# First convolution taps on ScalarE, and keys and up products on tiles without the norm's root, in a two-model kernel of exact fp32 products

## The chip, the cores and the metric

The kernel runs on one core of a Trainium2 chip. The metric is the device time in microseconds of one execution; a profiled execution also gives the span from the first to the last instruction. TensorE (PE) multiplies, VectorE (DVE), ScalarE (ACT) and GpSimd (POOL) do the rest, and SyncE (SP) issues the weights' transfers.

## The reference, cut to what matters

Two models are computed one behind the other on 256 tokens of width 1024. The first has two layers, each with a mixer (multi-head latent attention, then a short convolution) and a mixture of 32 experts, of which every token takes two:

```python
def expert_block(args):
    xb, e = args
    return (jax.nn.silu(xb @ w_gate[e]) * (xb @ w_up[e])) @ w_down[e]
```

The second has a state-space mixer and a dilated attention, each followed by an FFN with a causal depthwise convolution of width 3 over the tokens. The attention's keys and values come from a norm of their own:

```python
def _rms_norm(x, w, eps=RMS_EPS):
    xf = x.astype(jnp.float32)
    y = xf * lax.rsqrt(jnp.mean(xf * xf, axis=-1, keepdims=True) + eps)
    return (y * w.astype(jnp.float32)).astype(x.dtype)

def _conv_ffn(h, w_up, conv_w, w_down):
    u = _causal_depthwise_conv(h @ w_up.astype(h.dtype), conv_w)
    gate, val = u[..., :FFN_DIM], u[..., FFN_DIM:]
    return (jax.nn.silu(gate) * val) @ w_down.astype(h.dtype)

...
k_sh, v_sh = _shared_kv(x, kv_norm, w_kv, positions)
x = x + _dilated_mixer(_rms_norm(x, b_norm[j]), k_sh, v_sh, att_w_q[j], att_w_o[j], positions)
x = x + _conv_ffn(_rms_norm(x, ffn_norm[layer]), ffn_w_up[layer], ffn_conv_w[layer], ffn_w_down[layer])
```

## The kernel before

The program is a chain of stages, each a class with one method per engine: `Start`, `Mla`, `Moe` 0, `Conv`, `Moe` 1, `Ssm`, `Ffn` 0, `Dilated`, `Ffn` 1, `Finish`. Each engine runs its methods in the order in which the code is written; semaphores order the engines among each other. There is no scheduler.

The activations lie transposed in SBUF: `X` is 8 tiles of 128 features by the 256 tokens. Where fp32 must be exact, a value is split into a high part, rounded to the PE's fast format, and a low part, the rest; a product is then three fast products (high by high, low by high, high by low; `product3`, L584; `first_linear3_tensor`, L618 to L624). ACT rounds (`round_scalar`, L297) and DVE makes the rest (`rest_vector`, L303), for weights as for values. A weight chunk is 128 partitions by 4096 elements, and goes through a ring of six slots that SP fills in order; a slot is free when the products that read it are done.

A norm at a seam goes: DVE adds the stage's output to `X`, ACT squares (L432, L479), POOL adds squares up (L487), PE sums over partitions with ones (L495, L497), ACT takes the root (L652), DVE its reciprocal `rstd` (L657), then values times gain times `rstd` (L661), rounded by ACT (L680), lows by DVE (L668). Only then does the next stage's first product start.

`Moe`: after the routing's ranks (L1393) PE opens four accumulator banks with products of zeros (`open_tensor`, L1344), gathers the tokens of expert team 0 (L1307; its operands are the rounded turned x and its lows, L1578), and then takes the 32 experts in turn (gate and up L1328 and L1337, result L1352, into the accumulators). At the end comes a branch for experts with more tokens than fit, after which `more_begin` and so on would run.

`Ffn`: 11 up chunks, each two tiles m of 128 gate and 128 value columns. For each tile ACT evicts the products from PSUM (L2744 for the first two tiles, L2749 for the others) into `PB`, DVE does the convolution: first tap (L2783), two further taps (L2786), for both halves; ACT does the silu (L2726), POOL the product with the value half (L2808), ACT rounds it (L2728), POOL makes its low part (L2810). In `scalar` the steps stand in this order:

```python
for m in range(KFF):
    if m % 2 == 0:
        (self.w_up + self.w_down)[m // 2 + 1].round_scalar(e, w)
    if m >= 2:
        make_h(m - 2)
...
    if m >= 4:
        w.wait_ge(*dve.at(key, "taps", m - 4))
```

`make_h` is the silu, the wait for POOL's product and its rounding; the eviction of tile m comes behind it.

`Dilated`: keys of three pairs of heads (`keys`, from chunks `w_kv[0]`, `w_kv[1]`), values (`tokens`), rotary position turns (a PE product, L2894, then three DVE operations, L3130 to L3133), then the heads' queries, scores and outputs.

Of the kernel before, what the change touches and what calls it, by code (L numbers as in the profile page):

```python
# [16 lines left out]
P = 128  # L17
# [3 lines left out]
HALF = SLOT // 2  # L21

# [479 lines left out]
class Kernel:  # L502
# [102 lines left out]
    def first_linear3_tensor(self, e, w, chunk, outs, weights, values, n_k, tiles, pieces=False):  # L605
# [6 lines left out]
        for i in range(n_k):  # L612
# [4 lines left out]
            for out, name, cols in outs:  # L617
                e.matmul(out, high(i, cols).bitcast(F32R), values[0](i).bitcast(F32R), start=i == 0, stop=False)  # L618
                end = e.matmul(out, low(i, cols).bitcast(F32R), values[0](i).bitcast(F32R), start=False, stop=False)  # L619
        end.then_inc(*pe.up("free", chunk.number))  # L620
# [43 lines left out]
    def norm_parts_vector(self, e, w, tag, value, gain, high, low, chunk=None):  # L664
# [5 lines left out]
        for k in range(KD):  # L670
            self.norm_value_vector(e, w, tag, k, value, gain)
            if chunk and k % 2 and k > 1:
                chunk.rest_piece_vector(e, w, k // 2)
# [13 lines left out]
    def modulated_parts_vector(self, e, w, tag, layer, T, high, low, chunk=None):  # L687
# [9 lines left out]
        for k in range(KD):  # L697
# [3 lines left out]
            if chunk and k % 2 and k > 1:  # L701
                chunk.rest_piece_vector(e, w, k // 2)
# [514 lines left out]
class Moe:  # L1217
    def __init__(self, k, layer, T, cap, before):
# [12 lines left out]
        self.slots, self.zero = ar.take(P), ar.take(P)  # L1231
        self.zeros_by = k.mats[:, 0:4, :].rearrange("p m n -> p (m n)")
# [31 lines left out]
    def sync(self, e, w):  # L1264
# [8 lines left out]
        self.k.ring.close_halves()  # L1273
        self.more_sync(e, w)
# [81 lines left out]
    def tensor(self, e, w):  # L1356
# [38 lines left out]
        w.wait_ge(*pool.at(key, "zero"))  # L1395
        for b in range(KD // 2):
            _, emptied = banks.next(dve, key, "acc", b)
            banks.hold(key, "acc", b)
            w.wait_ge(*emptied)
        self.open_tensor(e)  # L1400
# [50 lines left out]
        for part in range(KD // 2):  # L1451
            gather(0, part)
        for x in range(EXPERTS):
# [21 lines left out]
    def scalar(self, e, w):  # L1475
# [52 lines left out]
        self.then.first_chunk().round_piece_scalar(e, w, 0)  # L1528
        k.root_scalar(e, w, ("moe", layer), SEQ, eps=NORM_EPS * NORM_EPS if layer else NORM_EPS)
        self.then.first_chunk().round_piece_scalar(e, w, 1)  # L1530
        act.mark("end", key)

    def vector(self, e, w):
# [144 lines left out]
        for part, between in enumerate((weights, shared, tables, lambda: self.last_steps.close_vector(e, w))):  # L1678
            turned_x(0, part)
            between()  # L1680
# [10 lines left out]
        for x in range(EXPERTS):  # L1691
# [7 lines left out]
            if x % TEAM == TEAM - 1 and x // TEAM + 2 < EXPERTS // TEAM:  # L1699
                places_of(x // TEAM + 2)  # L1700
        w.wait_ge(*pe.at(key, "sum", EXPERTS - 1))
# [5 lines left out]
        self.then.first_chunk().rest_piece_vector(e, w, 0)  # L1707
# [1671 lines left out]
```

## Time and profile before

| what | value |
| --- | --- |
| median of 3 runs | 2243.75 us (2243.53 to 2244.0) |
| profiled execution, its own time | 2242.49 us |
| its span | 2240.7 us, mean granted TensorE clock 0.975 |
| PE busy | 2109.5 us (94%) |
| DVE busy | 1003.7 us (45%) |
| ACT busy | 718.4 us (32%) |
| POOL busy | 244.7 us (11%) |

The shares are averages over the whole program. The stages differ: the expert stages move weights nearly all the time, the FFNs keep DVE as busy as PE. The expert stages end at about 742 and 1348 us, the first FFN's up chunks run from 1644 to 1773, the attention from 1844 to 2031, and the second FFN's up chunks to 2166.

### The profile page before, as it was taken

The numbers are of one execution on the slowest core, as the hardware profiler recorded it, in microseconds if no ns is written. First come the engines' busy times: TensorE is split into PE (matmuls) and PEld (weight loads), VectorE is DVE, ScalarE is ACT, GpSimd is POOL, SyncE is SP. The second block draws the span as 40 slices with busy tenths as digits, with TensorE's granted clock in tenths as the row PEclk, the third lists the DMA queues.
The fourth block names the chain that finished last, engine by engine and source line by source line (L and its number), as shares of the span: only waits on it lengthen the run. The fifth ranks groups of instructions, "written<-read, shape, count | busy, mean of one in ns | idle before, by whom it ended". The sixth has DMA issues, their size and how long they took to land. (4 is left out here: it accounts for less than half of the span.)

```text
span 2240.7 us, 31183 instructions
## 1 busy us (share of the span) xinstructions
PE 2109.5 (94%) x13462; PEld 1481.8 (66%) x13462; DVE 1003.7 (45%) x1653; ACT 718.4 (32%) x1079; POOL 244.7 (11%) x220
## 2 busy tenths in 40 slices
PE   5999999999999898999999988997899989998998
PEld 3845744444443696444444437975899989998997
DVE  3434411111111564111111107865479846777983
ACT  3234211111111442111111118855545534444552
POOL 0000000000000000000000000046125400002540
PEclk9999899999999999999999999999999999999999
DMA  9777599999999557999999985432345454434542
GB/s 326 252 273 275 227 410 421 421 421 421 421 421 421 192 204 304 417 421 421 422 420 421 421 352 191 151 113 76 113 151 189 174 196 122 113 113 151 188 171 94
DMA packets 216208, 616.86 MB, mean 275 GB/s; under 512 B 20224, under 2 KB 107392, under 8 KB 166656
## 3 DMA queue, kind: packets, MB, share of 16 engines
q1 hardware_dynamic: 208960, 612.01, 71.0%
q10 hardware_dynamic: 7104, 2.76, 0.5%
q8 instruction: 110, 1.80, 0.3%
q14 instruction: 34, 0.28, 0.0%
HBM read 613.69 MB, written 1.05 MB: 274 GB/s over the span
## 5 line engine op out<-in xcount | busy, mean ns | idle before, releaser
L1328 PE MATMUL bank<-ring,arena 128*64 128x512 f32 x2048 | 454.4, 593 | 12.4 <-DMA ring<-in_moe_w_up 12.3
L584 PE MATMUL bank<-normed_rounded,ring_rounded 128*128 128x256 f32 x3424 | 415.5, 283 | 5.0 <-ACT normed_rounded L680 3.4
L584 PEld LDWEIGHTS bank<-normed_rounded,ring_rounded 128*128 128x128 f32 x3424 | 411.2, 189 | 6.9 <-issue 4.3
L1328 PEld LDWEIGHTS bank<-ring,arena 128*64 128x64 f32 x2048 | 149.4, 137 | 305.8 <-issue 304.9
L1674 DVE TENSOR_TENSOR arena<-arena,bank 64x512 f32<-64x512 f32 x64 | 43.6, 681 | 659.3 <-ACT arena L1498 659.3
L303 DVE TENSOR_TENSOR ring_rounded<-ring,ring_rounded 128x4096 fp32r<-128x4096 f32 (+2 forms) x66 | 286.6, 4345 | 115.2 <-ACT ring_rounded L297 115.0
L584 PE MATMUL bank<-arena_rounded,ring_rounded 128*128 128x256 f32 x2336 | 290.9, 284 | 6.8 <-ACT arena_rounded L1927 2.6
L584 PEld LDWEIGHTS bank<-arena_rounded,ring_rounded 128*128 128x128 f32 x2336 | 283.3, 190 | 9.2 <-ACT arena_rounded L1927 3.4
L297 ACT ACTIVATE ring_rounded<-ring 128x4096 fp32r<-128x4096 f32 (+2 forms) x66 | 227.7, 3450 | 39.4 <-DMA ring<-in_ffn_w_down 32.8
L1337 PE MATMUL bank<-ring,arena 128*64 128x512 f32 x1024 | 233.8, 598 | 3.8 <-ACT arena L1505 3.8
L1498 ACT ACTIVATE arena<-bank 64x512 f32<-64x512 f32 x64 | 38.1, 596 | 451.0 <-PE bank L1328 451.0
L1337 PEld LDWEIGHTS bank<-ring,arena 128*64 128x64 f32 x1024 | 67.8, 136 | 122.4 <-issue 109.6
L572 PEld LDWEIGHTS bank<-mats,arena 128*128 128x128 f32 (+2 forms) x662 | 85.0, 167 | 78.8 <-issue 66.5
L1352 PE MATMUL bank<-arena 64*128 64x256 f32 x1024 | 127.8, 388 | 1.4 <-ACT arena L1512 1.4
L1512 ACT ACTIVATE arena<-bank 128x512 f32<-128x512 f32 x64 | 38.3, 599 | 275.2 <-PE bank L1337 275.2
L572 PE MATMUL bank<-mats,arena 128*128 128x128 f32 (+2 forms) x662 | 102.9, 278 | 8.5 <-POOL arena L2414 5.4
L1352 PEld LDWEIGHTS bank<-arena 64*128 64x128 f32 x1024 | 93.2, 186 | 23.7 <-issue 11.6
L2786 DVE SCALAR_TENSOR_TENSOR arena<-arena,cols 128x256 f32<-128x256 f32 x176 | 94.4, 537 | 6.3
L2810 POOL TENSOR_TENSOR arena_rounded<-arena,arena_rounded 128x256 fp32r<-128x256 f32 x44 | 93.5, 2125 | 23.3 <-ACT arena_rounded L2728 23.3
L1307 PE MATMUL bank<-arena_rounded 128*128 128x256 f32 x512 | 78.4, 298 | 0.0
L1307 PEld LDWEIGHTS bank<-arena_rounded 128*128 128x128 f32 x512 | 65.7, 190 | 5.0 <-issue 1.2
L1505 ACT ACTIVATE arena<-bank 128x256 f32<-128x256 f32 x64 | 24.7, 386 | 132.5 <-PE bank L572 132.5
(274 smaller groups left out, 2101.4 us busy)
## 6 DMA issues: line engine op xcount, KB each, us to landing
ring<-in_moe_w_gate SPq DMA_DIRECT2D x128, 1024.0 KB, 16.6
ring<-in_moe_w_up SPq DMA_DIRECT2D x128, 1024.0 KB, 18.7
ring<-in_moe_w_down SPq DMA_DIRECT2D x128, 1024.0 KB, 18.4
ring<-in_w_mod SPq DMA_DIRECT2D x24, 2048.0 KB, 11.8
ring<-in_ffn_w_up SPq DMA_DIRECT2D x44, 1024.0 KB, 6.9
ring<-in_ssm_w_in SPq DMA_DIRECT2D x12, 2048.0 KB, 8.3
ring<-in_ffn_w_down SPq DMA_DIRECT2D x10, 2048.0 KB, 8.0
ring<-in_conv_w_in SPq DMA_DIRECT2D x6, 2048.0 KB, 9.1
```

The costliest lines, as they stand in the source:

```text
L297: e.activation(ring.rounded[(self.number + 1) % RING][:, 0:n].bitcast(F32R), ring.slots[self.number % RING][:, 0:n], ACT.Copy).then_inc(*s ...
L303: e.tensor_tensor(ring.rounded[slot][:, 0:n].bitcast(F32R), ring.slots[slot][:, 0:n], ring.rounded[(self.number + 1) % RING][:, 0:n], ALU. ...
L572: return e.transpose(out, in_, self.mats[0:rows, 0, 0:rows])
L584: end = e.matmul(out, lhs.bitcast(F32R), rhs.bitcast(F32R), start=start and n == 0 and k == 0, stop=stop and n == 2 and k == n_k - 1)
L1307: end = e.matmul(out, f[:, t, feats].bitcast(F32R), mine[:, t, hot].bitcast(F32R), start=t == 0 and f is self.f_high, stop=t == self.NT - ...
L1328: ends[i] = e.matmul(bank[rows, :], xt[:, n * KD // 2 + j, :], weights[:, j, :], start=n == 0 and j == 0, stop=n == 1 and j == KD // 2 - 1)
L1337: end = e.matmul(bank[n * cap:(n + 1) * cap, :], self.ht[x][:, k, :], weights[:, i, n * 512:(n + 1) * 512], start=k == 0, stop=k == KF - 1)
L1352: end = e.matmul(self.acc(kk), self.y[x][rows, i * P:(i + 1) * P], self.back[x][rows, :], start=False, stop=last and kk % 2 == 1)
L1512: e.activation(self.y[x % 2], banks.of(key, "y", x)[:, :], ACT.Copy).then_inc(*act.up(key, "y", x))
L1674: e.tensor_tensor(h, h, banks.of(key, "h", x)[0:cap, :], ALU.mult).then_inc(*dve.up(key, "h", x))
L2786: e.scalar_tensor_tensor(buf, self.PB[:, s, j, q:q + T], w3[:, q:q + 1], buf, ALU.mult, ALU.add).then_inc(*dve.up())
L2810: e.tensor_tensor(self.H_low[:, m, :].bitcast(F32R), self.H[:, m, :], self.H_high[:, m, :], ALU.subtract).then_inc(*pool.up(key, "h low", m))
```

## The change

Five edits.

1. **Opening of the experts.** The zero products use a rounded zero (one fast pass each instead of several) and stand behind the gathers; DVE makes all turned tiles of team 0 before the routing weights.
2. **End of the experts.** The next stage's first chunk is fetched before the branch, ACT rounds its pieces 0 and 1 before the squares, DVE makes their rests around them. The loop for overfull experts is one loop instead of three.
3. **Seams into both FFNs.** The first two up chunks multiply `raw` = X times gain, without the root. Their rows take `rstd` at the eviction, which DVE does (`normed`). The sum of squares is closed inside the first product.
4. **First tap of the convolution** by ACT, after the eviction, as a copy with a scale per partition.
5. **Dilated attention.** The keys and values multiply raw tiles as well; keys take `rstd` at their eviction (`normed(n)`), values a scale by token (`by_token`), which PE turns from `rstd` (`roots`).

```diff
@@ Moe.tensor @@
-        w.wait_ge(*pool.at(key, "zero"))
...
-        self.open_tensor(e)
...
         for part in range(KD // 2):
             gather(0, part)
+        w.wait_ge(*pool.at(key, "zero"))
...
+        self.open_tensor(e)
@@ Moe.open_tensor @@
+        zero = self.zero_rounded.bitcast(F32R)
         for b in range(KD // 2):
-            e.matmul(self.k.banks.of(self.key, "acc", b)[:, :], self.zero, self.zeros_by, start=True, stop=False)
+            e.matmul(self.k.banks.of(self.key, "acc", b)[:, :], zero, across(zero, BANK // P), start=True, stop=False)
@@ Moe.scalar @@
+        for q in (0, 1):
+            self.then.first_chunk().round_piece_scalar(e, w, q)
...
         self.more_scalar(e)
-        self.then.first_chunk().round_piece_scalar(e, w, 0)
         k.root_scalar(e, w, ("moe", layer), SEQ, eps=NORM_EPS * NORM_EPS if layer else NORM_EPS)
-        self.then.first_chunk().round_piece_scalar(e, w, 1)
@@ Ffn.raw_vector @@
+    def raw_vector(self, e, w, m):
+        e.tensor_scalar(self.raw[:, m, :], k.X[:, m, 0:SEQ], k.col("ffn_norm")[:, self.layer, m:m + 1], None, ALU.mult
+                        ).then_inc(*k.dve.up(self.key, "raw value", m))
...
@@ Ffn.tensor @@
-        k.first_linear3_tensor(e, w, first, outs, (high, low), self.x_parts, KD, k.norm_tiles(key))
+        k.first_linear3_tensor(e, w, first, outs, (high, low), self.raw_parts, KD, self.raw_ready,
+                               between=lambda i: self.prior.close_tensor(e, w) if i == 1 else None)
@@ Ffn.scalar @@
-            if m % 2 == 0:
+            if m == 0:
+                self.w_up[2].round_scalar(e, w)
+            elif m % 2 == 0 and m > 2:
                 (self.w_up + self.w_down)[m // 2 + 1].round_scalar(e, w)
             if m >= 2:
                 make_h(m - 2)
...
+            w.wait_ge(*(act if m >= 4 else dve).at(key, "up", m))
+            for j in range(2):
+                e.activation(self.acc[:, s, j, :], self.PB[:, s, j, 0:T], ACT.Copy,
+                             scale=taps[:, self.layer, j * KFF + m, 0:1]).then_inc(*act.up(key, "tap", m, j))
@@ Ffn.vector @@
+            w.wait_ge(*act.at(key, "tap", m))
             for j in range(2):
                 buf, w3 = self.acc[:, s, j, :], taps[:, self.layer, j * KFF + m, :]
-                e.tensor_scalar(buf, self.PB[:, s, j, 0:T], w3[:, 0:1], None, ALU.mult).then_inc(*dve.up())
@@ Dilated.tensor @@
-        keys(0, False)
-        keys(1, True)
+        first_keys()
+        roots()
+        last_keys()
         rotary(("k", 0))
-        keys(2, False)
         rotary(("k", 1))
         tokens(self.w_kv[1], slice(256, 512), 0)
         rotary(("k", 2))
@@ Dilated.vector @@
-        self.w_kv[1].rest_vector(e, w)
         rotary(("k", 0))
+        rotary(("k", 1))
         self.w_kv[2].rest_vector(e, w)
-        rotary(("k", 1))
+        normed(2)
         rotary(("k", 2))
```

On ACT, in the FFN's loop (one weight chunk's rounding at L297, then two tiles), the rows before are:

```order
L297 ACTIVATE ring_rounded<-ring 128x4096
L2726 ACTIVATE arena<-arena 128x256
L2728 ACTIVATE arena_rounded<-arena 128x256
L2749 ACTIVATE arena<-bank 128x2x256
L2726 ACTIVATE arena<-arena 128x256
L2728 ACTIVATE arena_rounded<-arena 128x256
L2749 ACTIVATE arena<-bank 128x2x256
```

and after, where the rounding has line 298, silu 2783, rounding of the product 2785 and the eviction 2802:

```order
L298 ACTIVATE ring_rounded<-ring 128x4096
L2783 ACTIVATE arena<-arena 128x256
L2785 ACTIVATE arena_rounded<-arena 128x256
L2802 ACTIVATE arena<-bank 128x2x256
L2806 ACTIVATE arena<-arena,cols 128x256 x2
L2783 ACTIVATE arena<-arena 128x256
L2785 ACTIVATE arena_rounded<-arena 128x256
L2802 ACTIVATE arena<-bank 128x2x256
L2806 ACTIVATE arena<-arena,cols 128x256 x2
```

Behind every eviction stand two copies with a column as scale, ahead of the next silu; nothing else in the loop has moved.

On PE, at the opening of an expert stage, behind the ranks, before and after (L1344 and L1350 are the zero products, L1307 and L1312 the gather, L1328 and L1333 the first expert's gate and up):

```order
L1390 MATMUL bank<-arena,mats 128x32
L1393 MATMUL bank<-arena,mats 128x32 x2
L1344 MATMUL bank<-mats,arena 128x512 x4
L1307 MATMUL bank<-arena_rounded 128x256 x32
L1328 MATMUL bank<-ring,arena 64x512 x16
```

```order
L1396 MATMUL bank<-arena,mats 128x32
L1399 MATMUL bank<-arena,mats 128x32 x2
L1312 MATMUL bank<-arena_rounded 128x256 x32
L1350 MATMUL bank<-arena_rounded 128x512 x4
L1333 MATMUL bank<-ring,arena 64x512 x16
```

The gather has changed places with the zero products.

On DVE, at the entry of the dilated attention (L3130 to L3133 before and L3278 to L3281 after are a rotary, L303 and L304 the rest of a weight chunk, L3257 and L3262 after are `normed`), before and after:

```order
L668 TENSOR_TENSOR normed_rounded<-normed,normed_rounded 128x256 x8
L661 SCALAR_TENSOR_TENSOR arena<-residual,cols,rstd 128x256 x8
L668 TENSOR_TENSOR arena_rounded<-arena,arena_rounded 128x256 x8
L303 TENSOR_TENSOR ring_rounded<-ring,ring_rounded 128x4096
L3130 TENSOR_TENSOR residual<-bank,residual 32x2x256
L3131 TENSOR_TENSOR arena<-arena,residual 32x512
L3133 TENSOR_TENSOR arena<-arena,residual 32x512
L303 TENSOR_TENSOR ring_rounded<-ring,ring_rounded 128x4096
L3130 TENSOR_TENSOR residual<-bank,residual 32x2x256
L3131 TENSOR_TENSOR arena<-arena,residual 32x512
L3133 TENSOR_TENSOR arena<-arena,residual 32x512
L3130 TENSOR_TENSOR residual<-bank,residual 32x2x256
```

```order
L304 TENSOR_TENSOR ring_rounded<-ring,ring_rounded 128x4096
L3257 TENSOR_TENSOR arena<-bank,rstd 128x256 x4
L3268 COPY arena<-bank 128x2
L3278 TENSOR_TENSOR residual<-bank,residual 32x2x256
L3279 TENSOR_TENSOR arena<-arena,residual 32x512
L3281 TENSOR_TENSOR arena<-arena,residual 32x512
L3278 TENSOR_TENSOR residual<-bank,residual 32x2x256
L3279 TENSOR_TENSOR arena<-arena,residual 32x512
L3281 TENSOR_TENSOR arena<-arena,residual 32x512
L304 TENSOR_TENSOR ring_rounded<-ring,ring_rounded 128x4096
L3262 TENSOR_TENSOR arena<-bank,rstd 128x512
L3278 TENSOR_TENSOR residual<-bank,residual 32x2x256
```

The lows of the queries (L668 before, L3318 after) stand behind the rotaries now, and `normed(2)`, L3262, stands between the third chunk's rest and the third rotary.

## Rows read from the trace of the kernel before

**Rows 1.** The page's costliest groups (busy us, mean ns, idle before, releaser).
```profile
L1328 PE MATMUL bank<-ring,arena 128*64 128x512 f32 x2048 | 454.4, 593 | 12.4 <-DMA ring<-in_moe_w_up 12.3
...
L2786 DVE SCALAR_TENSOR_TENSOR arena<-arena,cols 128x256 f32<-128x256 f32 x176 | 94.4, 537 | 6.3
```

**Rows 2.** Timeline (start, duration, engine line op), PE, two openings of the experts.
```profile
264.79 6.65 PE L1344 MATMUL bank<-mats,arena 128*128 128x512 f32 x8 [1.90 <-DVE arena_rounded L1578]
270.87 4.47 PE L1307 MATMUL bank<-arena_rounded 128*128 128x256 f32 x32
...
870.33 5.96 PE L1344 MATMUL bank<-mats,arena 128*128 128x512 f32 x8 [1.90 <-DVE arena_rounded L1578]
```

**Rows 3.** Windows (PE, PEld, DVE, ACT, POOL busy, PE clock, DMA share, GB/s), first opening.
```profile
265.00:270.00 5.00, 5.00 (x6) 1.94 (x7) 0.44 (x3) 0.00 (x0) 0.00 (x0) 0.50 1.01 423
270.00:275.00 5.00, 5.00 (x34) 4.25 (x33) 2.40 (x7) 0.00 (x0) 0.00 (x0) 0.92 0.13 54
```

**Rows 4.** Timeline, ACT, the ends of the first and second expert stage.
```profile
746.37 1.28 ACT L312 ACT_TABLE_LOAD   x1 [0.79 <-issue]
...
1354.22 1.06 ACT L312 ACTIVATE ring_rounded<-ring 128x1024 fp32r<-128x1024 f32 x1 [1.38 <-DMA ring<-in_ssm_w_in]
```

**Rows 5.** Timeline, PE, from the state-space stage into the first FFN.
```profile
1639.99 0.70 PE L497 MATMUL bank<-rstd,mats 128*128 128x256 f32 x2 [0.53 <-ACT rstd L479]
...
1658.08 2.18 PE L584 MATMUL bank<-normed_rounded,ring_rounded 128*128 128x256 f32 x17
```

**Rows 6.** Timeline, ACT, DVE, POOL, the FFN loop's first cycle.
```profile
1658.56 3.62 ACT L297 ACTIVATE ring_rounded<-ring 128x4096 fp32r<-128x4096 f32 x1
1667.28 0.42 ACT L2728 ACTIVATE arena_rounded<-arena 128x256 fp32r<-128x256 f32 x1 [3.36 <-POOL arena L2808]
1670.17 3.63 ACT L297 ACTIVATE ring_rounded<-ring 128x4096 fp32r<-128x4096 f32 x1
...
1662.21 4.42 DVE L303 TENSOR_TENSOR ring_rounded<-ring,ring_rounded 128x4096 fp32r<-128x4096 f32 x1
...
1663.99 3.25 POOL L2808 TENSOR_TENSOR arena<-arena 128x256 f32<-128x256 f32 x1 [19.07 <-ACT arena L2726]
1668.56 0.74 POOL L2808 TENSOR_TENSOR arena<-arena 128x256 f32<-128x256 f32 x1
```

**Rows 7.** Windows, the first FFN's up chunks; timeline, DVE and POOL, a later cycle.
```profile
1658.00:1772.00 114.00, 114.00 (x963) 113.96 (x961) 109.44 (x133) 60.00 (x72) 65.74 (x40) 1.00 0.52 170
...
1731.64 4.97 DVE L303 TENSOR_TENSOR ring_rounded<-ring,ring_rounded 128x4096 fp32r<-128x4096 f32 x1
1743.09 4.97 DVE L303 TENSOR_TENSOR ring_rounded<-ring,ring_rounded 128x4096 fp32r<-128x4096 f32 x1
...
1732.86 4.35 POOL L2810 TENSOR_TENSOR arena_rounded<-arena,arena_rounded 128x256 fp32r<-128x256 f32 x1 [0.53 <-ACT arena_rounded L2728]
```

**Rows 8.** Timeline, PE, the first FFN's down products begin; ACT, a scaled copy.
```profile
1772.94 3.31 PE L584 MATMUL bank<-arena_rounded,ring_rounded 128*128 128x256 f32 x26 [0.78 <-ACT arena L2749]
...
1372.37 0.51 ACT L2324 ACTIVATE arena<-arena,cols 128x256 f32<-128x256 f32 x1
```

**Rows 9.** Timeline, PE and DVE, from the first FFN into the dilated attention.
```profile
1829.28 10.30 PE L584 MATMUL bank<-arena_rounded,ring_rounded 128*128 128x256 f32 x72 [2.11 <-DVE residual L2795]
1844.65 15.55 PE L584 MATMUL bank<-normed_rounded,ring_rounded 128*128 128x256 f32 x96 [3.40 <-ACT normed_rounded L680]
1873.14 1.02 PE L2894 MATMUL bank<-arena 128*128 128x512 f32 x2
...
1874.20 0.68 DVE L3130 TENSOR_TENSOR residual<-bank,residual 32x512 f32<-32x512 f32 x1 [3.30 <-PE bank L2894]
```

**Rows 10.** Timeline, PE, the entry of the second FFN and its down products.
```profile
2019.41 11.55 PE L584 MATMUL bank<-normed_rounded,ring_rounded 128*128 128x256 f32 x96
2051.05 2.18 PE L584 MATMUL bank<-normed_rounded,ring_rounded 128*128 128x256 f32 x17
...
2165.90 2.37 PE L584 MATMUL bank<-arena_rounded,ring_rounded 128*128 128x256 f32 x18 [0.78 <-ACT arena L2749]
```

More of the change, by code:

```diff
@@ L1677, in vector @@
             self.last_steps.step_vector(e, w, at)
-        for part, between in enumerate((weights, shared, tables, lambda: self.last_steps.close_vector(e, w))):
+        for part in range(KD // 2):
             turned_x(0, part)
-            between()
+        weights()
+        shared()
+        tables()
+        self.last_steps.close_vector(e, w)
         w.wait_ge(*dve.now())
@@ new lines, in more_tensor @@
+            with e.Fori(0, (self.n_blocks - 1) * EXPERTS, 1) as it:
+                e.wait_ge(*self.more_count("vector", it, 2))
+                awake()
+                for tile in range(KD):
+                    self.gather_tensor(e, x_turned[:, tile * self.cap:(tile + 1) * self.cap], tile, slice(0, self.cap),
+                                       self.mine[0])
+                self.back_tensor(e, turned, 0).then_inc(matmul, 1)
+                e.wait_ge(*self.more_count("vector", it, 4))
+                awake()
+                e.wait_ge(*self.more_count("landed", it, 48))
+                awake()
+                for half in range(2):
+                    tiles = slice(half * KD // 2, (half + 1) * KD // 2)
+                    end = self.gate_up_tensor(e, rows, self.rows_of(0), half, gate[:, tiles, :], up[:, tiles, :])[1]
+                end.then_inc(matmul, 1)
+                e.wait_ge(*self.more_count("vector", it, 5))
+                awake()
+                self.turn_h_tensor(e, turned, 0).then_inc(matmul, 1)
+                e.wait_ge(*self.more_count("scalar", it, 2))
+                awake()
+                self.down_tensor(e, x_turned, 0, range(KF), down).then_inc(matmul, 1)
+                e.wait_ge(*self.more_count("scalar", it, 3))
+                awake()
+                self.open_tensor(e)
+                self.sum_tensor(e, 0, True).then_inc(matmul, 1)
+                e.wait_ge(*self.more_count("vector", it, 6))
+                awake()
@@ new lines, in roots, with last_keys @@
+        def roots():
+            bank, emptied = banks.next(dve, "att root")
+            w.wait_ge(*emptied)
+            w.wait_ge(*dve.at("root", ("ffn out", 0)))
+            for c in range(2):
+                end = k.turn(e, bank[:, c * P:(c + 1) * P], k.rstd[:, c * P:(c + 1) * P])
+            end.then_inc(*pe.up("att root"))
+        def last_keys():
+            chunk = self.w_kv[1]
+            (high,), (low,) = chunk.high(), chunk.low()
+            bank, emptied = banks.next(dve, "pair", ("k", 2))
@@ L2909, in keys @@
-            if last:
-                pe.mark("free", chunk.number)
+                                  self.k_parts, KD, chunk.ready())
+            ends[2].then_inc(*pe.up("pair", ("k", 2)))
         def query(h, g):
@@ L3193, in vector @@
             k.plain_vector(e, w, "att y", m)
+            self.then.raw_vector(e, w, m)
+        for m in range(4):
+            self.then.raw_low_vector(e, w, m)
         self.then.prepare_vector(e, w)
@@ L3196, in vector @@
             k.plain_vector(e, w, "att y", m)
-        k.root_vector(e, w, "dilated out", T)
+            self.then.raw_vector(e, w, m)
+        for m in range(4, KD):
+            self.then.raw_low_vector(e, w, m)
+        for q in range(4):
+            if q == 2:
+                k.root_vector(e, w, "dilated out", T)
+            self.then.w_up[1].rest_piece_vector(e, w, q)
         dve.mark("end", "dilated")
```

256 lines of the change are left out of this document (167 added, 89 removed).

## The prediction

> **What bounds the kernel now.** I read the page's totals first, then the timelines around each place that the diff touches, then the windows of the FFN. TensorE is busy for 94% of the span (the table above), and its costliest group, the experts' gate products, idles 12.4 us, nearly all for a transfer [rows 1]: the expert stages run at the pace of the DMA late and of TensorE early, and everything else is a TensorE stage with short waits at its seams. So only two things can move the time: the seams (norms, openings), and whatever could take the FFN's up chunks away from TensorE.
>
> The FFN is the place to look at closely. Over its 114 us of up chunks PE is busy 114.00 and DVE 109.44, while ACT has 60.00 and POOL 65.74 [rows 7]. Two engines run level: one cycle (one weight chunk, two tiles) takes DVE 1743.09 - 1731.64 = 11.45 us, and PE 96 products at 11.55/96 = 0.12 us [rows 10], 11.4 to 11.5. That ACT is half idle does not mean that it has room. Its program order per tile is silu, wait for POOL's product, round the product, evict the next tile, and once a cycle a weight chunk's rounding. In the first cycle of the loop (starts 1658.56 and 1670.17) this serial chain alone takes 11.61 us [rows 6]. The reader is to see why: ACT's rounding ends, DVE starts the chunk's rest at 1662.21 for 4.42, and POOL's product, issued at 1663.99, ends only at 1667.24, 0.61 behind the rest. Unhindered the same product takes 0.74. So ACT waits 3.36 us behind a DVE operation that it has itself released [rows 6]. Later in the loop DVE is late by its own load, and the operation caught under the rest is POOL's next one, 4.35 us [rows 7].
>
> The Trainium skill says this too (SBUF — State Buffer, "Who interferes with whom"): a DVE instruction with two SBUF inputs and a GpSimd instruction that reads SBUF exclude each other for a whole instruction, and issue order decides who waits. The 4.42-us rest and the 3.25-us product agree with it.
>
> **The change, part by part.**
>
> Opening of the experts, twice. Before, PE waits 1.90 for the shared lows, does eight records of plain fp32 zeros for 6.65 us at half the clock (0.50), and only then the gather, 4.47 [rows 2, 3]. After, the gather starts as soon as its operands are there (265.3, the same release plus the copies) and runs 4.47 at full, up to 8.9 at half clock; I take a start at half clock and 6.4. Then four rounded zero products of 512 columns, twice a 256-column one: 4 x 0.24 = 0.95. That ends at 272.65, against 270.87 + 4.47 = 275.3 [rows 2]: -2.6. The second opening, 5.96 of zeros, by the same steps: -2.3. Bounds of each: 0 (the expert stream is the transfers' from there on) and -4.6 (full clock). The DMA share falls to 0.13 in the window behind the opening [rows 3], so the transfers have been waiting for slots which the products free, and move along with them; hence not 0.
>
> End of the experts, twice. A table load of 1.28 and a rounded piece of 1.06 leave the chain between squares and root [rows 4]; in their place two pieces precede the squares, which then start about 0.95 later: -1.4. At the second stage the piece also waited 1.38 for its transfer [rows 4], which now starts earlier: -2.8. Bounds: -3.7 and +1.
>
> Entries of the two FFNs. Today the root must be complete before the first product, and the first chunk ends at 1658.08 [rows 5] and 2051.05 [rows 10]. After, the products follow the out products at once. Into the first FFN: start 1639.95, 96 products 11.45, and between them the closing squares, which today end at 1639.99 + 0.70 [rows 5] and take 1.9 with their waits: 1653.3, -4.8. Into the second: out products end at 2030.96 [rows 10], + 11.55 + 1.5: 2044.05, -7.0. The 16 added raw operations per seam lie on DVE and ACT under the out products; they delay the first chunk's rest by up to 3.4 us, which the start above includes. If they cost more, the gain falls one for one.
>
> Entry of the dilated attention. The 3.40 wait and the slow products behind it (15.55 for 96, where 11.55 is the full-clock time) [rows 9, 10] go: the first keys end at 1851.7 instead of 1860.04. Then comes a new wait. DVE's order is now rotary 0, rotary 1, the rest of the third chunk, `normed(2)`, and TensorE's third rotary needs that last one. From PE's first rotary at 1857.8 (the first keys' 1851.7, the root's transposes 0.3, 48 products 5.8): two rotaries of three operations of 0.68 each (4.1; the first of today's third one stands in [rows 9]), a rest of 4.42 as in [rows 6], 0.7: 1867.9 against 1873.14 [rows 9], with TensorE idle for about 2.8. Net -5.5, between -8.3 (no wait) and -4. The tokens queued behind this rotary on PE move with it.
>
> First taps of the FFN, 44 each, from DVE to ACT. DVE loses four `TENSOR_SCALAR` a cycle. On ACT a copy with a scale column on such a tile takes 0.51 [rows 8], 0.48 of it beyond the overlap of neighbours: four a cycle are 1.92, and all of them stand in the serial chain, behind the eviction and ahead of the next silu. And relieving DVE does not take the POOL wait away, it fixes it: DVE's cycle work falls to 4.42 + 8 x 0.54 = 8.7 us [rows 1, 6], so DVE is always idle when ACT's rounding ends, its rest starts 0.03 later, and ACT's silu needs 0.4 before POOL may even start. So every cycle is as the first one of today, 11.61, plus 1.92: **13.53 us** against 11.4 of PE. TensorE, which had nothing to wait for, waits 2.1 us per chunk.
>
> For the first FFN: the rounding of the fourth up chunk ends at 1672.9 (today 1670.17 + 3.63 = 1673.8 [rows 6]). Seven cycles later, 1767.6, the last up chunk is rounded; from there to the eviction that releases the down products are one more cycle and 6.1 us, so they start at 1787.3, against 1772.94 [rows 8]: +14.35, the better entry included. The second FFN by the same steps: 2064.1 + 94.7 + 19.7 = 2178.5 against 2165.90 [rows 10]: +12.6. Behind that point nothing on the path changes.
>
> **The sum.** Openings -4.9, ends -4.2, first FFN +14.35, attention -5.5, second FFN +12.6: +12.35. The profiled execution took 2242.49, so 2254.8; the median of the runs lies 1.26 higher, so about **2256 us**. A measurement of this kernel tells about 0.2%, 4.5 us.
>
> **Rivals.**
> 1. *TensorE stays the bound in the FFNs (faster).* DVE is at 109 of 114 us and ACT at 60 [rows 7]; if only load counted, moving work from the one to the other would be free. It needs POOL's product to get in ahead of the rest. Then the chain loses about 3.4 a cycle, is 10.1, and PE sets 11.4. The time would be -9.1 - 4.8 - 5.5 - 7.0 = -26.4: 2217. Against it: the order rest, then product, is seen in [rows 6] exactly where DVE was idle. The Trainium skill speaks for this rival in words (Perfetto Trace Analysis, "Optimizing Scalar/DVE Operations": where DVE is saturated, some work may go to Scalar). By that sentence the sum would be 2217 as well; by the rows it is 2256.
> 2. *A cycle in between (no change).* Fourteen cycles count, so each 0.1 us of cycle is 1.4 us, and the sum is zero at 13.53 - 12.35/14 = 12.65 us. Taps that overlap the evictions, or some cycles of each kind, would do it: 2239 to 2248.
> 3. *TensorE loses its clock too (slower still).* Waits of 2 to 3 us have cost it: after one of 3.40 the 96 products took 4.0 more than at full clock [rows 9, 10]. With every chunk at 14.5 the sum is +12.35 + 14 x 1.0 = +26: 2270. Up to 2.1 us of it are free, since PE would only fill its own wait.
> 4. *The seams don't give what I count (slower).* If the raw operations make the out products' evictions late, -4.8 and -7.0 are lost: the FFN cycles are untouched by that only if the fourth rounding is late as well, which adds up to 10 us: 2266.
>
> **How the numbers follow.** The forecast's own case (cycle 13.1 to 14.0, seams as counted) 0.55, giving 2248 to 2264; rival 3 0.10; rival 4 0.07; rival 2 0.10; rival 1 0.18. Slower by over 0.2% is 0.55 + 0.10 + 0.07, within 0.2% 0.10, faster 0.18. The range leaves out rival 1's lower part and the end of rival 3: 2230 to 2268.
>
> **What would show it.** In the FFN of the changed kernel: DVE's 4.42-us rests 13.5 us apart with idle time before each, ended by ACT's rounding; POOL's `TENSOR_TENSOR` beside each of them at about 4.7 instead of 0.8; ACT waiting on POOL 4.7 once a cycle; PE with a wait of about 2 us per chunk; the first down product near 1778 in the new trace's time (9.1 earlier seams taken off 1787). Rests 11.4 apart with PE busy throughout would make the forecast wrong, and so would a POOL product of 0.8 that ends before the rest starts. At the attention's third rotary PE should idle nearly 3 us for DVE; at both openings the gather should start within 0.5 us of the shared lows, and the zeros take about 1 us.

## The result, and the profile after

| | before | after |
| --- | --- | --- |
| median | 2243.64 us (4 runs) | 2261.69 us (4 runs, 2258.08 to 2262.1) |
| ratio, 95% interval | | 1.008 (1.0062 to 1.0097) |
| profiled execution's span | 2240.7 us | 2259.9 us |

The changed kernel is 18 us slower, 0.8%. The forecast was 2256 in a range to 2268, slower. The page of the changed kernel, two of the costliest groups (busy us, mean ns, idle before, releaser):

```profile
L585 PE MATMUL bank<-normed_rounded,ring_rounded 128*128 128x256 f32 x3136 | 384.7, 284 | 23.9 <-DVE ring_rounded L304 22.4
...
L2896 POOL TENSOR_TENSOR arena<-arena 128x256 f32<-128x256 f32 x44 | 99.4, 2259 | 133.8 <-ACT arena L2783 133.8
```

TensorE's products on normed values now idle 22.4 us for DVE's rests; before, the same group idled 5.0, 3.4 of it for ACT:

```profile
L584 PE MATMUL bank<-normed_rounded,ring_rounded 128*128 128x256 f32 x3424 | 415.5, 283 | 5.0 <-ACT normed_rounded L680 3.4
```

POOL's product with the value half averages 2.26 us, three times its free 0.74 [rows 6].

In the changed kernel the rest of a weight chunk is L304, POOL's product L2896, its low part L2898, and the matrix products are L585. The experiments' kernels have their own numbers, some lines on from the kernel that each starts from; there DVE's rest in pieces is L312 or L313.

The FFN's cycle, timeline of ACT, DVE, POOL and PE in the changed kernel, and the start of the down products:

```profile
1675.18 3.61 ACT L298 ACTIVATE ring_rounded<-ring 128x4096 fp32r<-128x4096 f32 x1
1683.88 0.42 ACT L2785 ACTIVATE arena_rounded<-arena 128x256 fp32r<-128x256 f32 x1 [4.79 <-POOL arena L2896]
1688.64 3.61 ACT L298 ACTIVATE ring_rounded<-ring 128x4096 fp32r<-128x4096 f32 x1
...
1678.82 4.43 DVE L304 TENSOR_TENSOR ring_rounded<-ring,ring_rounded 128x4096 fp32r<-128x4096 f32 x1 [1.47 <-ACT ring_rounded L298]
1692.28 4.42 DVE L304 TENSOR_TENSOR ring_rounded<-ring,ring_rounded 128x4096 fp32r<-128x4096 f32 x1 [1.47 <-ACT ring_rounded L298]
...
1679.17 4.68 POOL L2896 TENSOR_TENSOR arena<-arena 128x256 f32<-128x256 f32 x1 [4.38 <-ACT arena L2783]
1686.11 0.75 POOL L2896 TENSOR_TENSOR arena<-arena 128x256 f32<-128x256 f32 x1 [1.00 <-ACT arena L2783]
...
1683.30 11.65 PE L585 MATMUL bank<-normed_rounded,ring_rounded 128*128 128x256 f32 x96 [1.79 <-DVE ring_rounded L304]
...
1779.33 20.90 PE L585 MATMUL bank<-arena_rounded,ring_rounded 128*128 128x256 f32 x155 [5.54 <-ACT arena L2802]
```

This is the picture which the forecast asked for. ACT rounds at 1675.18 and 1688.64: 13.46 us a cycle. Its rounding ends at 1678.79, DVE starts the rest 0.03 later, POOL's product starts at 1679.17 and takes 4.68, ending 0.60 behind the rest; ACT stands for 4.79 us. The second product of the cycle, beside no rest, takes 0.75. PE waits 1.79 for the next chunk, and 5.54 ahead of the down products (0.78 before [rows 8]).

The early seams, timeline of PE: the first opening, the first product of the convolution, and a late stretch of that stage:

```profile
263.85 6.38 PE L1312 MATMUL bank<-arena_rounded 128*128 128x256 f32 x32 [2.41 <-DVE arena_rounded L1584]
270.06 1.09 PE L1350 MATMUL bank<-arena_rounded 128*128 128x512 f32 x4
271.08 7.09 PE L1333 MATMUL bank<-ring,arena 128*64 128x512 f32 x32
...
747.07 0.55 PE L619 MATMUL bank<-normed_rounded,ring_rounded 128*128 128x256 f32 x1 [4.24 <-ACT normed_rounded L714]
...
821.25 23.49 PE L585 MATMUL bank<-arena_rounded,ring_rounded 128*128 128x256 f32 x185 [0.28 <-ACT arena_rounded L1937]
```

The gather has its 6.4 us, the zeros 1.09, as costed. From the ranks' products to the first expert it is 271.08 - 260.83 = 10.25 us against 275.27 - 261.85 = 13.42: -3.2. The other opening gives -1.5, the two ends -2.35 and -1.65 by the same reading. The last row is one that gave some back: these 185 products took 21.94 us before, now 23.49. The granted clock from 820 to 830 us is 0.83 now; before, every window over the same products shows 1.00.

From the state-space stage into the first FFN, timeline of PE and ACT:

```profile
1600.18 30.56 PE L585 MATMUL bank<-arena_rounded,ring_rounded 128*128 128x256 f32 x256 [0.41 <-DVE ring_rounded L304]
1641.09 3.95 PE L627 MATMUL bank<-arena_rounded,ring_rounded 128*128 128x256 f32 x32
...
1661.73 3.61 ACT L298 ACTIVATE ring_rounded<-ring 128x4096 fp32r<-128x4096 f32 x1
```

The out products end at 1630.74 (1639.02 before), the first up chunk at 1645.04 (1658.25 before; the row behind it in [rows 5] starts 0.17 before that end): 13.2 us ahead, of which 8.3 were there at the out products and 4.9 are the seam's. The fourth chunk's rounding ends at 1665.34 (1673.80 by [rows 6]).

Into and through the dilated attention's entry, timeline of PE and DVE:

```profile
1838.04 10.30 PE L585 MATMUL bank<-arena_rounded,ring_rounded 128*128 128x256 f32 x72 [2.19 <-DVE residual L2877]
1856.64 3.96 PE L627 MATMUL bank<-normed_rounded,ring_rounded 128*128 128x256 f32 x32
1876.98 2.08 PE L3000 MATMUL bank<-arena 128*128 128x512 f32 x2 [2.55 <-DVE arena L3262]
...
1871.92 4.41 DVE L304 TENSOR_TENSOR ring_rounded<-ring,ring_rounded 128x4096 fp32r<-128x4096 f32 x1
1876.25 0.67 DVE L3262 TENSOR_TENSOR arena<-bank,rstd 128x512 f32<-128x512 f32 x1
```

The first keys end at 1860.60, 12.3 behind the last out product (20.6 before, by [rows 9]). The third rotary waits 2.55 for `normed(2)`, which DVE reaches only when the rest of 4.41 is through.

The second FFN's entry (last products of the attention) and down products, timeline of PE; and a window behind the first FFN's long wait (PE, PEld, DVE, ACT, POOL busy, PE clock, DMA share, GB/s):

```profile
2023.42 11.55 PE L585 MATMUL bank<-normed_rounded,ring_rounded 128*128 128x256 f32 x96
...
2183.39 64.46 PE L585 MATMUL bank<-arena_rounded,ring_rounded 128*128 128x256 f32 x528 [5.55 <-ACT arena L2802]
...
1780.00:1790.00 10.00, 10.00 (x69) 10.00 (x69) 6.48 (x8) 5.18 (x9) 3.22 (x4) 0.77 0.21 66
```

The down products start at 2183.39 (2165.90 before [rows 10]) behind 5.55 us of waiting, and 528 of them take 64.46 where they took 62.77. In the window behind the first such wait the mean granted clock is 0.77: part of the window at the lower of the two levels of 1.2 and 2.4 GHz, part at the higher.

How far PE is ahead of the kernel before (-) or behind (+), from the starts and ends above and those of before:

| point | us | part of it | forecast |
| --- | --- | --- | --- |
| end of the state-space stage's products | -8.3 | openings -4.7, ends -4.0, rest of the way +0.4 | -9.1 |
| first FFN's down products start | +6.4 | +14.7 | +14.35 |
| their end | +8.8 | +2.4, of it 2.3 in slower products | none |
| attention's last products end | +4.0 | -4.75 | -5.5 |
| second FFN's down products start | +17.5 | +13.5 | +12.6 |
| end | +19.2 | +1.7 | none |

### The profile page after: what moved, and what is told of

It is laid out like the page before. It is cut to its first block and busy times, and to the rows that moved or that the text cites. A ratio compares the mean times of both kernels' runs of the same rounds, so it can differ in the third digit from the quotient of the medians.

```text
span 2259.9 us, 31244 instructions
## 1 busy us (share of the span) xinstructions
PE 2107.6 (93%) x13456; PEld 1484.2 (66%) x13456; DVE 982.9 (43%) x1621; ACT 752.7 (33%) x1172; POOL 242.5 (11%) x222
## 5 line engine op out<-in xcount | busy, mean ns | idle before, releaser
L1333 PE MATMUL bank<-ring,arena 128*64 128x512 f32 x2048 | 454.3, 593 | 11.9 <-DMA ring<-in_moe_w_up 11.8
L585 PE MATMUL bank<-normed_rounded,ring_rounded 128*128 128x256 f32 x3136 | 384.7, 284 | 23.9 <-DVE ring_rounded L304 22.4
L585 PEld LDWEIGHTS bank<-normed_rounded,ring_rounded 128*128 128x128 f32 x3136 | 378.2, 190 | 27.6 <-DVE ring_rounded L304 25.8
L1333 PEld LDWEIGHTS bank<-ring,arena 128*64 128x64 f32 x2048 | 149.3, 137 | 305.7 <-issue 304.3
L585 PE MATMUL bank<-arena_rounded,ring_rounded 128*128 128x256 f32 x2528 | 317.9, 286 | 16.4 <-ACT arena L2802 11.1
L304 DVE TENSOR_TENSOR ring_rounded<-ring,ring_rounded 128x4096 fp32r<-128x4096 f32 (+1 forms) x64 | 269.2, 4206 | 131.6 <-ACT ring_rounded L298 131.6
L585 PEld LDWEIGHTS bank<-arena_rounded,ring_rounded 128*128 128x128 f32 x2528 | 310.2, 193 | 18.8 <-ACT arena L2802 11.4
L298 ACT ACTIVATE ring_rounded<-ring 128x4096 fp32r<-128x4096 f32 (+1 forms) x64 | 220.4, 3443 | 44.4 <-DMA ring<-in_ffn_w_down 36.2
L2866 DVE SCALAR_TENSOR_TENSOR arena<-arena,cols 128x256 f32<-128x256 f32 x176 | 102.0, 579 | 54.4 <-ACT arena L2806 48.8
L2896 POOL TENSOR_TENSOR arena<-arena 128x256 f32<-128x256 f32 x44 | 99.4, 2259 | 133.8 <-ACT arena L2783 133.8
L1358 PEld LDWEIGHTS bank<-arena 64*128 64x128 f32 x1024 | 93.3, 186 | 23.7 <-issue 11.6
L1312 PE MATMUL bank<-arena_rounded 128*128 128x256 f32 x512 | 82.3, 310 | 4.8 <-DVE arena_rounded L1584 4.8
L1312 PEld LDWEIGHTS bank<-arena_rounded 128*128 128x128 f32 x512 | 70.0, 203 | 8.8 <-DVE arena_rounded L1584 5.1
L321 DVE TENSOR_TENSOR ring_rounded<-ring,ring_rounded 128x1024 fp32r<-128x1024 f32 x44 | 58.5, 1344 | 24.9 <-ACT ring_rounded L313 24.7
## 6 DMA issues: line engine op xcount, KB each, us to landing
ring<-in_w_mod SPq DMA_DIRECT2D x24, 2048.0 KB, 11.4
ring<-in_conv_w_in SPq DMA_DIRECT2D x6, 2048.0 KB, 12.6
```

Of the source, the lines that this page charges most:

```text
L298: e.activation(ring.rounded[(self.number + 1) % RING][:, 0:n].bitcast(F32R), ring.slots[self.number % RING][:, 0:n], ACT.Copy).then_inc(*s ...
L304: e.tensor_tensor(ring.rounded[slot][:, 0:n].bitcast(F32R), ring.slots[slot][:, 0:n], ring.rounded[(self.number + 1) % RING][:, 0:n], ALU. ...
L321: e.tensor_tensor(ring.rounded[slot][:, cols].bitcast(F32R), ring.slots[slot][:, cols], ring.rounded[(self.number + 1) % RING][:, cols], A ...
L585: end = e.matmul(out, lhs.bitcast(F32R), rhs.bitcast(F32R), start=start and n == 0 and k == 0, stop=stop and n == 2 and k == n_k - 1)
L1312: end = e.matmul(out, f[:, t, feats].bitcast(F32R), mine[:, t, hot].bitcast(F32R), start=t == 0 and f is self.f_high, stop=t == self.NT - ...
L1333: ends[i] = e.matmul(bank[rows, :], xt[:, n * KD // 2 + j, :], weights[:, j, :], start=n == 0 and j == 0, stop=n == 1 and j == KD // 2 - 1)
```

## The experiments

Theory: ACT's work in the FFN loop is a serial chain which holds one POOL product shut out for the length of a DVE rest; the taps lengthen this chain beyond PE's 11.4 us. Rivals: the seams' new work is what slows the FFN; the mere count of ACT's instructions does; the taps are covered. Each median is given with the ratio to the kernel before on the same chip and its interval. In those comparisons the kernel before had medians of 2242.2 to 2243.1.

**1. The taps back on DVE**, in the changed kernel.

```diff
-            w.wait_ge(*act.at(key, "tap", m))
             for j in range(2):
+                w.wait_ge(*dve.now())
+                e.tensor_scalar(buf, self.PB[:, s, j, 0:T], w3[:, 0:1], None, ALU.mult).then_inc(*dve.up())
```

> The changed kernel with the FFN's first taps back on DVE, all else kept. The theory (ACT's serial chain with the locked POOL product sets the cycle, and the taps lengthen it): the cycle falls from 13.46 to 11.4-11.6 us, 14 cycles give about 27 us and the two waits of 5.5 us ahead of the down products shrink to about 1, so 2222 to 2230. The rival that the seams (raw tiles, evictions by DVE) are what lengthens the FFN: the cycle stays above 13, and the time falls by under 5 us, 2257 to 2262.

Measured: 2236.03, 0.9975 (0.9963 to 0.9987). Two of DVE's rests, and the start of the down products on PE:

```profile
1684.51 4.97 DVE L304 TENSOR_TENSOR ring_rounded<-ring,ring_rounded 128x4096 fp32r<-128x4096 f32 x1
1696.38 4.97 DVE L304 TENSOR_TENSOR ring_rounded<-ring,ring_rounded 128x4096 fp32r<-128x4096 f32 x1
...
1772.97 7.28 PE L585 MATMUL bank<-arena_rounded,ring_rounded 128*128 128x256 f32 x59 [2.29 <-ACT arena L2802]
```

The 13.46-us cycle is gone, which refutes the seams as its cause; but the time is 6 to 14 us over what I expected. DVE's rests stand 11.87 us apart and the down products still wait 2.29. My edit had an extra wait of DVE on itself ahead of each tap (0.12 us each, 0.48 a cycle), and DVE is full here.

**5. The same without that wait** (it stays for the four tiles that DVE itself evicts).

> As the first experiment, but without the wait that I had put ahead of each first tap (DVE waited for its own last result; it cost 0.12 us for each tap, 0.48 a cycle, and made DVE's cycle 11.87). The theory: DVE's cycle is 11.45 again and the time 5 to 8 us below the 2236.0 of the first experiment, 2227 to 2231. If 2236 was due to something else than DVE's cycle, it stays within 2 us of it.

Measured: 2230.50, 0.9947 (0.9929 to 0.9965), inside. PE:

```profile
1674.61 92.97 PE L585 MATMUL bank<-normed_rounded,ring_rounded 128*128 128x256 f32 x752 [3.45 <-DVE ring_rounded L304]
1768.36 21.89 PE L585 MATMUL bank<-arena_rounded,ring_rounded 128*128 128x256 f32 x183 [0.78 <-ACT arena L2802]
```

The down products wait 0.78 again. What is left at the loop's entry is a wait of 3.45 (3.20 in the second FFN) for DVE at the loop's start, where DVE has taps and the new evictions together. This is 12.6 us under the kernel before: the change without its taps is a gain. Inside the 752 products the row shows no wait; in the second FFN they took 91.02, 11.6 per 96.

**2. The taps alone**, on top of the kernel before: the two ACT copies per tile, DVE's `tensor_scalar` gone.

> The kernel before with the first taps on ACT and nothing else of the change. The theory: cycle 13.5 us, 14 to 16 cycles of 2.0 us and two exit waits of about 5, so 2275 to 2285, the worst of all. The rival (taps on ACT are covered by ACT's idle time): 2243 to 2246.

Measured: 2284.90, 1.0186 (1.0157 to 1.0215), inside, just under its upper end. A chunk of the loop, and the down products, on PE:

```profile
1710.42 11.66 PE L584 MATMUL bank<-normed_rounded,ring_rounded 128*128 128x256 f32 x96 [1.80 <-DVE ring_rounded L303]
...
1793.02 56.77 PE L584 MATMUL bank<-arena_rounded,ring_rounded 128*128 128x256 f32 x456 [5.54 <-ACT arena L2750]
```

The cycle is 13.46 here too, though nothing of the seams is in this kernel, and the same two waits, 1.80 and 5.54, stand on PE. Alone the taps cost 42.7 us by the medians, more than the 31.2 between experiment 5 and the changed kernel. In the changed kernel they also have something to give: with them the wait at the first loop's start is 0.17, and without them, in experiment 5, 3.45. The two FFNs' waits of that kind (3.45 and 3.20) are over half of the difference.

**3. The rests in quarters**, in the changed kernel.

```diff
             elif m % 2 == 0 and m > 2:
-                (self.w_up + self.w_down)[m // 2 + 1].rest_vector(e, w)
+                (self.w_up + self.w_down)[m // 2 + 1].rest_quarters_vector(e, w)
...
+        for q in range(4):
+            cols = slice(q * n // 4, (q + 1) * n // 4)
+            e.tensor_tensor(ring.rounded[slot][:, cols].bitcast(F32R), ring.slots[slot][:, cols],
+                            ring.rounded[(self.number + 1) % RING][:, cols], ALU.subtract
```

> The changed kernel, where DVE makes the rest of each up chunk in the FFN's loop in four instructions of a quarter instead of one. The theory (POOL's product is shut out for the length of one DVE instruction): it gets in behind the first or second quarter, ACT's wait of 4.78 us falls to 1.2-2.5, the cycle to between 11.4 and 11.9, the time to 2225 to 2238. The rival that ACT is simply loaded or that POOL is shut out until DVE has an empty queue: the wait stays at 4.8 or grows by the 0.5 us which four instructions cost more, 2262 to 2270.

Measured: 2223.45, 0.992 (0.989 to 0.995), a little under the range. ACT, DVE, POOL and PE:

```profile
1685.56 3.61 ACT L298 ACTIVATE ring_rounded<-ring 128x4096 fp32r<-128x4096 f32 x1
1691.07 0.42 ACT L2794 ACTIVATE arena_rounded<-arena 128x256 fp32r<-128x256 f32 x1 [1.59 <-POOL arena L2905]
1696.95 3.62 ACT L298 ACTIVATE ring_rounded<-ring 128x4096 fp32r<-128x4096 f32 x1
...
1689.20 6.28 DVE L313 TENSOR_TENSOR ring_rounded<-ring,ring_rounded 128x1024 fp32r<-128x1024 f32 x4 [1.09 <-ACT ring_rounded L298]
...
1689.55 1.48 POOL L2905 TENSOR_TENSOR arena<-arena 128x256 f32<-128x256 f32 x1 [5.44 <-ACT arena L2792]
...
1764.60 54.30 PE L594 MATMUL bank<-arena_rounded,ring_rounded 128*128 128x256 f32 x456 [0.78 <-ACT arena L2811]
```

ACT makes every instruction that it made before, taps included, and DVE takes longer for the rest (6.28 for four quarters beside POOL). Yet POOL's product, issued 0.35 behind the first quarter, is through in 1.48, ACT waits 1.59 for it, the cycle is 11.39 and PE's. Neither the count of ACT's instructions nor DVE's load is the cause; the length of one DVE instruction is.

**9. The rests in halves**, to see the size of the effect follow the size of the instruction.

> The changed kernel with the up rests in two halves of 2.2-2.3 us in place of one instruction of 4.42 or of four. The theory (POOL is shut out until the DVE instruction in progress ends): POOL's product, 4.67 whole and 1.48 with quarters, takes 2.4 to 2.9, ACT's wait about 2.8, the cycle 11.4 to 11.6, the time 2222 to 2228. If splitting helped in some other way (a lighter DVE queue), the product would take about 1.5 as with quarters, or stay at 4.7.

Measured: 2235.53, 0.9965 (0.9951 to 0.9979). POOL and PE:

```profile
1703.12 2.55 POOL L2905 TENSOR_TENSOR arena<-arena 128x256 f32<-128x256 f32 x1 [4.38 <-ACT arena L2792]
1706.21 2.21 POOL L2907 TENSOR_TENSOR arena_rounded<-arena,arena_rounded 128x256 fp32r<-128x256 f32 x1 [0.53 <-ACT arena_rounded L2794]
...
1707.88 11.66 PE L594 MATMUL bank<-normed_rounded,ring_rounded 128*128 128x256 f32 x96 [0.30 <-DVE ring_rounded L313]
1767.85 22.35 PE L594 MATMUL bank<-arena_rounded,ring_rounded 128*128 128x256 f32 x174 [2.40 <-ACT arena L2811]
```

The product takes 2.55, between 4.68 whole and 1.48 in quarters, as the theory has it. The time is 7.5 us over the expected range: the second half now catches POOL's next operation (2.21 at 1706.21; 0.73 beside no DVE instruction in the changed kernel), which delays the second product; the cycle is 11.95 and the down products wait 2.40. I had counted one lock a cycle where halves have two. And behind the wait of 2.40 the 456 down products take 55.72 us, 1.4 more than in experiment 3 behind 0.78.

**4. ACT's order turned**: evictions and taps of both tiles run beside the rest, the products come behind it.

```diff
+        for m in range(4, KFF, 2):
+            (self.w_up + self.w_down)[m // 2 + 1].round_scalar(e, w)
+            evict(m)
+            evict(m + 1)
...
+            make_h(m - 2)
+            make_h(m - 1)
```

> The changed kernel with ACT's order in the FFN's loop turned: rounding, then eviction and taps of both tiles, then silu and product of the two tiles of the cycle before. Same instructions, same engines; the eviction and taps (3.0 us) now run while DVE makes the rest. The theory: the chain is 3.6 + 5.1 + 0.4 + 0.4 + 0.8 + 0.4, about 10.8 us, so PE sets the cycle at 11.4: 2216 to 2228. The rival that the number of ACT's instructions is what counts: 13.4 and 2260 to 2263.

Measured: 2231.46, 0.9946 (0.993 to 0.9962), 3.5 us over the range. ACT, DVE, POOL, PE:

```profile
1689.57 3.61 ACT L298 ACTIVATE ring_rounded<-ring 128x4096 fp32r<-128x4096 f32 x1
1697.07 0.40 ACT L2783 ACTIVATE arena<-arena 128x256 f32<-128x256 f32 x1
...
1693.21 4.42 DVE L304 TENSOR_TENSOR ring_rounded<-ring,ring_rounded 128x4096 fp32r<-128x4096 f32 x1 [1.79 <-ACT ring_rounded L298]
...
1697.55 0.74 POOL L2902 TENSOR_TENSOR arena<-arena 128x256 f32<-128x256 f32 x1 [6.93 <-ACT arena L2783]
...
1697.69 23.05 PE L585 MATMUL bank<-normed_rounded,ring_rounded 128*128 128x256 f32 x192 [0.21 <-DVE ring_rounded L304]
1775.08 1.79 PE L585 MATMUL bank<-arena_rounded,ring_rounded 128*128 128x256 f32 x8 [3.02 <-ACT ring_rounded L313]
```

With the same instructions the cycle is 11.6 us (23.05 for two chunks, and 0.21 of waiting for DVE), and POOL's first product is issued at 1697.5, when DVE's rest is nearly over, and takes 0.74. The missing part is at the exit: the pieces of the second down chunk are now rounded late, PE waits 3.02 (and 0.42) for them in each FFN.

**8. Quarters in the kernel before**, where DVE is full.

> The kernel before with the FFN's up rests in four quarters, nothing else. There DVE is full and POOL's wait is off the path. The theory: quarters cost DVE 0.5 to 1.3 us a cycle and give nothing, the cycle is 11.9 to 12.7, the time 2248 to 2262. The rival that POOL's wait costs in the kernel before too: 2235 or less.

Measured: 2246.50, 1.0021 (1.0008 to 1.0034). DVE and PE:

```profile
1733.14 5.73 DVE L312 TENSOR_TENSOR ring_rounded<-ring,ring_rounded 128x1024 fp32r<-128x1024 f32 x4
1744.86 5.71 DVE L312 TENSOR_TENSOR ring_rounded<-ring,ring_rounded 128x1024 fp32r<-128x1024 f32 x4
...
1657.35 114.74 PE L593 MATMUL bank<-normed_rounded,ring_rounded 128*128 128x256 f32 x960
```

Slower, by less than expected: the rest goes from 4.97 to 5.73, but the DVE operations that stood beside POOL get shorter in return, and the quarters stand 11.7 us apart (1733.14 and 1744.86) where the rests stood 11.45 [rows 7]. PE takes 114.74 for 960 products without a wait that the row shows (114.08 before). The down products, which ran without a break before, wait 0.39 and 0.71 for DVE in the first FFN and 0.27 and 0.70 in the second; with 0.66 and 0.78 in the up chunks that is 3.5 us, the 3.4 that the medians differ by. The lock is there in the kernel before, off the path: shortening it gives nothing.

**10. Taps on ACT and quarters**, on top of the kernel before.

> The kernel before with the first taps on ACT (2284.9 in the second experiment) and the up rests in quarters. The theory: the 41 us which the taps cost there all come through the locked wait; with quarters the chain falls below PE's 11.4 and the time is that of before or a little less, 2238 to 2246. The rival that the taps' own 1.9 us a cycle on ACT cost something even so: 2250 or more.

Measured: 2243.58, 1.0003 (0.9989 to 1.0017), inside. ACT:

```profile
1725.22 3.62 ACT L297 ACTIVATE ring_rounded<-ring 128x4096 fp32r<-128x4096 f32 x1
1730.73 0.42 ACT L2737 ACTIVATE arena_rounded<-arena 128x256 fp32r<-128x256 f32 x1 [1.59 <-POOL arena L2820]
1736.61 3.62 ACT L297 ACTIVATE ring_rounded<-ring 128x4096 fp32r<-128x4096 f32 x1
```

The 42.7 us are gone; the cycle is 11.39 with taps and all. So the price of the taps went through the locked wait, to within this run's interval of about 3 us. But nothing is gained either: with TensorE at its bound, moving the taps buys no time in this kernel.

**6. The edits of the expert stages alone.**

> The kernel before with the edits of the expert stages alone (opening behind the gather, rounded zeros, the first chunk's pieces ahead of the squares, the earlier fetch). In the changed kernel PE is 7.3 us ahead at the state-space stage's first product and 4.8 at its last. The theory (real gain at each seam, partly given back by half-clock stretches that move): the final time is 3 to 7 us lower, 2235 to 2241. The rival that the expert stream's transfers take all of it back: within 1 us of before.

Measured: 2235.77, 0.9964 (0.9952 to 0.9975), inside, -7.3 us. PE, where the state-space stage's closing squares start, right behind its last products (1638.86 in the kernel before):

```profile
1630.87 0.60 PE L495 MATMUL bank<-arena,mats 128*128 128x256 f32 x2
```

8.0 us ahead there and 6.9 at the last closing squares (2222.16 against 2229.01): the gain stands and is not taken back by the transfers.

**7. Quarters, and `normed(2)` ahead of the rest**, the best version.

```diff
-        self.w_kv[2].rest_vector(e, w)
         normed(2)
+        self.w_kv[2].rest_vector(e, w)
         rotary(("k", 2))
```

> The third experiment (2223.5) with normed(2) ahead of the third key chunk's rest on DVE in the dilated attention. The theory: the wait of 2.5 us at the third rotary is DVE's order and nothing else, so it goes to under 0.3 and 2.2 to 2.6 us come off: 2220 to 2222. The rival: the rest is then late for the value products behind that rotary, and PE waits as long there: 2222 to 2225.

Measured: 2219.13, 0.9889 (0.9871 to 0.9907), 0.9 under the range and faster than both kernels. PE's third rotary and DVE:

```profile
1857.56 1.02 PE L3009 MATMUL bank<-arena 128*128 128x512 f32 x2
...
1855.87 4.40 DVE L304 TENSOR_TENSOR ring_rounded<-ring,ring_rounded 128x4096 fp32r<-128x4096 f32 x1
```

The rotary follows without a wait, and the value products behind it (at 1858.01) start on time. Its median is 4.3 us below the third experiment's, of which the order explains the 2.5 of the wait; the two intervals overlap, so the other 1.8 is not shown to be anything.

## Why the prediction was right

**The bound of the FFNs.** "Every cycle is as the first one of today, 11.61, plus 1.92": 13.46 was measured, 13.53 forecast. Every link was read in [rows 6]: the rest 0.03 behind the rounding, the product's end 0.6 behind the rest's. The first cycle of the kernel before holds a table load of 1.28 on ACT (at 1662.20) which the prediction doesn't name and later cycles don't have. It did no harm: POOL is issued later by it and waits less (3.25 for the product against 4.68), but its end is set by the rest's end in both. Experiments 3 and 9 show the link itself, 2 and 10 that the taps cost only through it, and 4 that the order in which ACT meets it is enough. The rival that load alone counts (2217) fails in the changed kernel. The Trainium skill's sentence for it (Perfetto Trace Analysis, "Optimizing Scalar/DVE Operations") is not borne out by the taps alone, 2284.90. Once the lock is shortened, the taps on ACT cost nothing in the kernel before (experiment 10, 2243.58), and the changed kernel with them (experiment 3, 2223.45) is 7 us by the medians under the one that has them on DVE with whole rests (experiment 5, 2230.50; the intervals touch). Experiment 7's 2219.13 lies near the rival's 2217, but holds the cut rests and another order on DVE, which the rival didn't ask for. What the Trainium skill says of the lock (SBUF — State Buffer, "Who interferes with whom") agrees with all of them, 4.68, 2.55 and 1.48 us for one product beside a whole, a half and a quarter rest.

**The two FFN terms.** +14.7 and +13.5 against +14.35 and +12.6. The first seam gave 4.9 (forecast 4.8), so the rival with late raw operations fell; the second gave 5.9 in place of 7.0.

**The attention.** -4.75 against -5.5: first keys -8.3 as forecast, new wait 2.55 (2.8). Experiment 7 shows its cause, DVE's order. The prediction's terms for the third rotary add up to 1867.0 and not to its 1867.9: it doesn't list PE's product ahead of DVE's first operation (1.06 by the starts in [rows 9]). The 10.1 us that it has from the first rotary to `normed(2)` are what came, 1866.79 to 1876.92. Against 1873.14 its 1867.9 is -5.2, and its -5.5 is -8.3 plus 2.8. Part of what is missing lies behind the new wait: two rotary products took 2.08 us there and the 48 behind them 12.71, against 1.02 and 11.71 before; in experiment 3, behind the same wait of 2.56, it was 1.12 and 11.76.

**The early seams.** Openings -4.7 (-4.9) and ends -4.0 (-4.2) in sum, though each single one was off by 0.6 to 1.2, in both directions; that the sums fit is luck. Experiment 6 has them alone at -7.3.

**The size.** The sum said +12.35, the span shows +19.2, over half as much again; the range held it, the sum didn't. The main missing term is the clock behind the waits ahead of the down products. I forecast where these start, and had a case for a lost clock, but placed it inside the up chunks, where PE has 2 us to spare per chunk (two chunks of the second FFN did run at 13.2 us instead of 11.65, and cost nothing). Behind the wait of 5.5 nothing is to spare: 456 products take 56.52 (54.23 before), 56.77 in experiment 2 with the same wait, 55.72 in experiment 9 with a wait of 2.40, 54.30 in experiment 3 with a wait of 0.78. In the second FFN 528 products cost 1.7 more. The two are 4.0 of the 6.8 us that the sum lacks; the other 2.8 are the single terms above.

## What to carry to other kernels

Before moving work to an engine that looks half idle, write down that engine's instructions in their order with what each waits for: a wait that is harmless while another engine sets the pace becomes the pace when the chain grows, and relieving the full engine can fix the wait in place. Where GpSimd and a long VectorE instruction meet, cut the VectorE instruction or issue other work beside it; on a full VectorE without such a chain the cut costs. And where a long wait of TensorE is new, add its slower products behind it: here 1.7 to 2.5 us behind each 5.5, and anything from 0.1 to 2 behind waits of about 2.5.

## What the runs showed of the hardware that was not expected

POOL's product gets in between two DVE instructions that stand back to back, in its turn: issued 0.35 us after the first quarter began, it was through 1.83 after that start, while DVE's four quarters took 6.28 us together, against 4.42 for the rest in one piece. Cutting does not end the exclusion; it moves part of its price from POOL to DVE, and pays where DVE has the time. And stretches at a lower granted clock don't stay where they were: the same 185 products of the convolution took 21.94 us in one kernel and 23.49 in the other with no wait of their own changed. That the change moved them isn't shown. Runs of the kernel before alone range from 2236.35 us at a mean clock of 0.979 to 2249.15 at 0.973, so a single trace says little about where such a stretch lies.
